# Matmuls over the unnormalised x ahead of four normalised stages of a two-block transformer forward pass

## The reference

```python
def rms(x, g):
    x32 = x.astype(jnp.float32)
    y = x32 * lax.rsqrt(jnp.mean(x32 * x32, axis=-1, keepdims=True) + EPS)
    return (y * g.astype(jnp.float32)).astype(x.dtype)
...
        merged = (gates[:, :, 0] * (y_fox @ w_proj_fox[l])
                  + gates[:, :, 1] * (y_s5 @ w_proj_s5[l])
                  + gates[:, :, 2] * (y_mem @ w_proj_mem[l]))
        x = x + merged @ w_out[l]
    return rms_norm(x, g_final)
...
    for l in range(DEPTH_2):
        ada = c_act @ w_ada[l] + b_ada[l]
        sh1, sc1, gt1, sh2, sc2, gt2 = [a[:, None, :] for a in jnp.split(ada, 6, axis=-1)]

        h = rms(x, g_mix[l]) * (1.0 + sc1) + sh1
        parts = jnp.split(h @ w_in[l], IN_SPLITS, axis=-1)
        ...
        y_a = gqa_attention(qa, ka, va) @ w_branch_a[l]
        ...
        y_b = dilated_attention(qs, kss, vs) @ w_branch_b[l]

        gate_a = jax.nn.sigmoid(parts[3 + 3 * N_B])
        gate_b = jax.nn.sigmoid(parts[4 + 3 * N_B])
        mixed = gate_a * y_a + gate_b * y_b
        x = x + gt1 * (mixed @ w_out[l])

        h2 = rms(x, g_mlp[l]) * (1.0 + sc2) + sh2
        x = x + gt2 * (jnp.square(jax.nn.relu(h2 @ w_ff1[l])) @ w_ff2[l])
```

## Time and profile before

| what | value |
|---|---|
| median of 3 timed executions | 2289.02 us (2288.14 to 2290.26) |
| the profiled execution, its own time | 2291.23 us |
| span of the profiled execution | 2289.4 us |
| mean granted clock of TensorE in it | 0.992 |
| TensorE busy, matmuls | 2249.8 us, 98% |
| GpSimd busy | 1691.9 us, 74% |
| VectorE busy | 1259.3 us, 55% |
| ScalarE busy | 632.8 us, 28% |
| chain of work that ended last | TensorE 85%, GpSimd 6%, VectorE 4%, issue 2%, ScalarE 2%, DMA 1% |
| moved by the DMA queues | 280.87 MB |

### The profile page before, as it was taken

How to read it: one execution, slowest core, us unless ns; L and a number is a source line. 1 busy time by engine, 2 the same in 40 slices (tenths; PEclk the granted TensorE clock), 3 DMA queues, 4 the chain that set the end, 5 groups by cost and what they waited for, 6 DMA issues and landing times.

```text
span 2289.4 us, 31094 instructions
## 1 busy us (share of the span) xinstructions
PE 2249.8 (98%) x11693; PEld 1828.1 (80%) x11693; DVE 1259.3 (55%) x1798; ACT 632.8 (28%) x1286; POOL 1691.9 (74%) x2678
## 2 busy tenths in 40 slices
PE   8999999999999999999999999999999999999999
PEld 6888677788887888777778888878877777888887
DVE  7986345554446665544867576457554456723221
ACT  3233344332224111543223233111144421300000
POOL 7998170867888798344889887889853387899884
PEclk9999999999999899999999999999999999999999
DMA  7456741334455332111545555533321132433221
GB/s 204 129 137 153 268 151 35 116 101 159 159 186 186 111 111 94 50 36 39 164 131 189 174 191 177 184 107 97 100 79 33 29 124 92 154 107 107 92 92 56
DMA packets 268656, 280.87 MB, mean 123 GB/s; under 512 B 29964, under 2 KB 240592, under 8 KB 268508
## 3 DMA queue, kind: packets, MB, share of 16 engines
q1 hardware_dynamic: 249756, 245.86, 34.8%
q10 hardware_dynamic: 18752, 33.03, 4.3%
HBM read 257.87 MB, written 17.85 MB: 120 GB/s over the span
## 4 chain that ended last, share of the span: by engine, by line
PE 85%; POOL 6%; DVE 4%; issue 2%; ACT 2%; DMA 1%; SPq 0%; ACTq 0%; DVEq 0%; POOLq 0%
PE ps L496 46%; PE ps L674 14%; PE ps L2527 4%; PE ps L2528 4%; PE ps L2529 4%; POOL ring_low L272 4%; POOL ring_high L268 3%; PE ps L982 2%; PE ps L1025 2%; PE ps L1001 2%; PE ps L1175 1%; PE ps L1182 1%; PE ps L1158 1%; PE ps L2637 1%; DVE ada_acc L408 1%
## 5 line engine op out<-in xcount | busy, mean ns | idle before, releaser
L272 POOL TENSOR_TENSOR ring_low<-ring,ring_high 128x256 fp32r<-128x256 f32 x1309 | 1039.0, 824 | 28.4
L268 POOL TENSOR_SCALAR ring_high<-ring 128x256 fp32r<-128x256 f32 x1309 | 609.1, 491 | 478.3 <-PE ps L674 170.8
L496 PE MATMUL ps<-hT_high,ring_high 128*128 128x512 f32 x704 | 278.0, 395 | 1.4 <-DVE hT_low L860 1.4
L496 PE MATMUL ps<-hT_low,ring_high 128*128 128x512 f32 x704 | 274.9, 390 | 0.0
L496 PE MATMUL ps<-hT_high,ring_low 128*128 128x512 f32 x704 | 274.0, 389 | 0.0
L674 PE MATMUL ps<-hT_high,ring_high 128*128 128x512 f32 x568 | 234.5, 413 | 3.2 <-POOL ring_low L272 1.4
L674 PE MATMUL ps<-hT_high,ring_low 128*128 128x512 f32 x568 | 225.3, 397 | 0.0
L674 PE MATMUL ps<-hT_low,ring_high 128*128 128x512 f32 x568 | 225.1, 396 | 0.0
L408 DVE TENSOR_REDUCE ada_acc<-ring 128x256 f32<-128x2048 f32 x48 | 188.8, 3933 | 54.8 <-ACT ring L395 54.7
L496 PE MATMUL ps<-hidden_high,ring_high 128*128 128x512 f32 x512 | 201.0, 393 | 0.0
L496 PE MATMUL ps<-hidden_low,ring_high 128*128 128x512 f32 x512 | 199.6, 390 | 0.0
(11 more groups left out here) (401 smaller groups left out, 4030.5 us busy)
## 6 DMA issues: line engine op xcount, KB each, us to landing
ring<-in_w_in_dram SPq DMA_DIRECT2D x75, 1024.0 KB, 5.3
ring<-in_w_ff_dram SPq DMA_DIRECT2D x64, 1024.0 KB, 5.4
ring<-in_w_ada_dram SPq DMA_DIRECT2D x48, 1024.0 KB, 5.4
ring<-in_w_out_dram SPq DMA_DIRECT2D x12, 1024.0 KB, 5.8
scratch_x<-xT ACTq DMA_DIRECT2D x3, 2048.0 KB, 8.2
ring<-in_w_mem_kv_dram SPq DMA_DIRECT2D x4, 1024.0 KB, 5.4
ring<-in_w_branch_a_dram SPq DMA_DIRECT2D x16, 256.0 KB, 4.0
xT<-scratch_x ACTq DMA_DIRECT2D x2, 2048.0 KB, 9.7
```

The source lines that it names most:

```text
L268: ins = nc.gpsimd.tensor_scalar(x(hi), x(raw), 1.0, 1.0, ALU.mult, ALU.mult)
L272: ins = nc.gpsimd.tensor_tensor(x(lo), x(raw), x(hi).bitcast(F32), ALU.subtract)
L496: return nc.tensor.matmul(out[0:rows, bank, cols[0]:cols[1]], lhsT, rhs, start=start, stop=stop)
```

## The change

A normalised and modulated x is `h = x * rstd * gain + shift`, with `rstd` a number per position and `gain` and `shift` numbers per feature. So `h @ W` is `rstd * ((x * gain) @ W) + shift @ W`. The change uses this for a few tiles of each normalised stage:

- During the output tiles in front of a norm, ScalarE rounds up `x * gain` (`Unnormed.round_up`) and VectorE makes its low part (`Unnormed.low_part`), slice by slice as x is updated, and both go into `hT`. One slice behind the last tile is done in the norm stage.
- In the norm stage TensorE works on tiles over this `hT`, 24 products each, and mixes in the products with the shift, 16 matmuls with two columns per tile (`shift_of`; `factors_ahead` makes the high and low part of the shift), the sums (now eight one-column matmuls over `sums` and `last`) and the transposes of the root. The `warm` matmuls are gone. The slices of `hT` are overwritten by the normalised ones when TensorE has used them (`used`). VectorE then multiplies the tiles by `rstd` (`take`).
- In front of layer 0's projections two tiles run ahead: both tiles of the first gate slab `m00ga`. In front of layer 1's, one tile of `m10ga`; the other one runs beside the first four slices of the first projection group, over the normalised x (`beside`). In both layers the gate slab moves ahead of the projections' slabs in the ring, and the stream has 14 gate tiles (336 products) instead of 16, with new paces. `turn_gates` does the tanh of the two at the start of the turn stage.
- In front of both feed-forwards tiles 0 and 1 of `w_ff1` run ahead; tiles 2 and 3 then go slice by slice (`done=2`). The temporary of the norm is in PSUM banks 4 and 6 there.
- The mixing stage waits for the last of the stream at its tile 3 instead of at its entry.
- Five modulation slabs of layer 0 come in the merge, behind the gate slabs with odd numbers 3 to 11, tied to half 0 of that slab; the first block's output stage has two instead of four, and layer 0's output stage none instead of three. The merge has `ada_lag=2` instead of 3.

```diff
@@ plan_slabs
-    def ada(l):
+    def ada(l, half=1):
...
-        key = (last, 1) if K.slabs[last][3] else (last, None)
+        key = (last, half) if K.slabs[last][3] else (last, None)
...
             add(f"merge{mp}{b}g", w, dm, O_GL + D * b, D, part=mp)
+            one = (len(K.slabs) - 1, 1)
+            if 3 * mp + b in (3, 5, 7, 9, 11):
+                ada(0, 0)
             add(f"merge{mp}{b}p", T[pw][0], (0, rows), 0, D, part=mp)
...
         add("out", T["w_out"][0], dm, 0, D, part=i)
-        ada(0)
+        if i < 2:
+            ada(0)
     for l in range(LAYERS):
         w2 = T["w_in_2"][l]
+        add(f"m{l}0ga", w2, dm, 3072, D, part=0)
...
             add(f"out{l}", T["w_out_2"][l], dm, 0, D, part=i)
-            if l == 0 and i < 3:
-                ada(0)
@@ tiles_stage
-                first = 2
+                first = 2 + done
...
-                    for n in range(2):
+                    for n in range(done, done + 2):
@@ new
+def factors_ahead(K, e, shift):
+    v, hi = K.nc.vector, K.shift_two[:, :, 0]
+    K.link(e, "dve_step", v.tensor_copy(hi, shift))
+    K.link(e, "dve_step", v.tensor_tensor(K.shift_two[:, :, 1], shift, hi.bitcast(F32), ALU.subtract))
+class Unnormed:
...
+    def round_up(self, e, k):
+
+        K = self.K
+        K.nc.scalar.activation(K.hT[0][:, k, :], self.src[:, k, :], ACT.Copy, scale=self.gain[:, k:k + 1]
+                               ).then_inc(self.high.sem, 1)
+
+    def low_part(self, e, k):
+
+        K = self.K
+        e.wait_ge(self.high.sem, self.base + k + 1)
+        K.nc.vector.scalar_tensor_tensor(K.hT[1][:, k, :], self.src[:, k, :], self.gain[:, k:k + 1],
+                                         K.hT[0][:, k, :].bitcast(F32), ALU.mult, ALU.subtract).then_inc(self.low.sem, 1)
@@ norm_stage
+            def products_of(k):
+                pe.wait_ge(unnormed.low.sem, unnormed.base + k + 1)
+                for n, t in enumerate(tiles):
+                    if k == 0:
+                        K.weight_here(pe, t[0][5])
+                    for x in range(3 * k, 3 * k + 3):
...
+            def shift_of(n, k):
+
+                for x in (3 * k, 3 * k + 2):
+                    ins = nc.tensor.matmul(ps[:, shift_bank, 2 * n:2 * n + 2], tiles[n][x][3], K.shift_two[:, k, :],
+                                           start=x == 0, stop=x == 3 * KD - 1)
...
+            pe.wait_ge(taken.sem, taken.total - 2)
+            for k in range(KD):
+                products_of(k)
+                if twice is not None:
+                    squared, summed = twice[0]
+                    for h in (2 * k, 2 * k + 1):
+                        shift_of(h // KD, h % KD)
+                    if k == 1:
+                        pe.wait_ge(taken.sem, taken.total)
+                        pe.wait_ge(summed.sem, summed.total)
+                        pe.wait_ge(squared.sem, squared.total - 1)
+                        turn(turn_bank, (sums, last))
+                    if k == 3:
+                        pe.wait_ge(inverted.sem, i0 + 1)
+                        spread_root(root_bank, 4)
+                    if k == 4:
+                        pe.wait_ge(squared.sem, squared.total)
+                        turn(other_bank, (twice[3], twice[4]))
+                    if k == 6:
+                        pe.wait_ge(inverted.sem, i0 + 2)
+                        spread_root(other_bank, 1)
+                else:
+                    for h in range(len(tiles) * k, len(tiles) * (k + 1)):
+                        shift_of(h // KD, h % KD)
+                    if k == (2 if len(tiles) == 1 else 1):
+                        pe.wait_ge(taken.sem, taken.total)
+                        turn(turn_bank, (sums, last))
+                    if k == (4 if len(tiles) == 1 else 2):
+                        pe.wait_ge(inverted.sem, i0 + 1)
+                        spread_root(root_bank, 4)
...
             def round_up(k):
                 e.wait_ge(scaled.sem, s0 + k + 1)
+                e.wait_ge(used.sem, u0 + k + 1)
...
+            K.link(e, "dve_step", v.tensor_copy(rstd[:, :], ps[:, root_bank, :]))
+            e.wait_ge(made.sem, made0 + len(tiles))
+            for n in range(len(tiles)):
+                K.link(e, "dve_step", v.tensor_reduce(K.shift_of[:, n:n + 1], ps[:, shift_bank, 2 * n:2 * n + 2], AX_X, ALU.add))
+                take(e, n, ps[:, tile_banks[n], :], rstd[:, :])
@@ qkv_stage
+                        if g == 0 and beside is not None and k < KD // 2:
+                            if k == 0:
+                                K.weight_here(pe, beside[0][0][5])
+                            for j in (2 * k, 2 * k + 1):
+                                pe.wait_ge(arriving[0].sem, arriving[1] + j + 1)
+                                for _, _, _, lhsT, rhs, _, start, stop in beside[0][3 * j:3 * j + 3]:
+                                    ins = nc.tensor.matmul(K.ps[:, beside[1], :], lhsT, rhs, start=start, stop=stop)
@@ layer
+    def turn_gates(e):
+        e.wait_ge(gates_scaled.sem, gates_scaled.total)
+        for n in range(2):
+            shift = {"bias": K.half_shift[:, n:n + 1]} if n < ahead else {}
+            nc.scalar.activation(gates[n], scaled_gates[n][:, :], ACT.Tanh, scale=0.5, **shift).then_inc(gates_turned.sem, 1)
...
-                    [72 + 9 * i for i in range(18)] + [240, 252])
+                    [72] + [85 + 8 * i for i in range(17)] + [220, 226])
...
-                         [(252, 252, 274)] + [(278 + 14 * i, 284 + 14 * i, 288 + 14 * i) for i in range(7)] + [(376, 382, 384)])
+                         [(226, 226, 246)] + [(249 + 10 * i, 254 + 10 * i, 256 + 10 * i + 8 * (i == 6)) for i in range(7)] + [(328, 334, 336)])
...
-    tiles_stage(K, tiles, 2, dve=mix_dve, also=mix_high, waits={(0, 0): (al.sem, al0 + 4), (0, 12): (yl.sem, yl0 + 2)})
+    tiles_stage(K, tiles, 2, dve=mix_dve, also=mix_high, tensor_entry={x: y for x, y in before.items() if x != "stream"},
+                entry_at=(3, {"stream": before["stream"]}), waits={(0, 0): (al.sem, al0 + 4), (0, 12): (yl.sem, yl0 + 2)})
...
-    tiles_stage(K, column_tiles(K, K.first[f"out{l}"], KD, KD, split), 1, dve=out_dve, ahead=mlp_gain,
+    tiles_stage(K, column_tiles(K, K.first[f"out{l}"], KD, KD, split), 1, dve=out_dve, also=out_high, ahead=mlp_gain,
                 arriving=(xl, xl0, before, 5))
...
+    after[5] = 1
...
     def ff_act(e, n, ps):
+        if n < 2:
+            e.wait_ge(first_scaled.sem, scaled0 + n + 1)
+            return nc.scalar.activation(rel[:, n, :], rel[:, n, :], ACT.Relu, bias=K.shift_of[:, n:n + 1])
```

## The result

The changed kernel takes 2303.84 us (2302.14 to 2306.41), against 2288.86 us before on the same chips: a ratio of 1.0063, 95% interval 1.0051 to 1.0075. It is 15 us slower where 7 us faster was forecast. Its profiled execution took 2306.41 us, with a span of 2304.6.

The account below looks back on a forecast made before the run. TensorE bounds (busy 2249.8 of 2289.4 us), GpSimd second. Terms 20.4 + 1.4 + 1.5 + 1.6 + 2.9 - 10.9 - 9.7 = 7.2 us faster, so 2281.8 us; 8 in 10 range 2270 to 2292.

Parts of the forecast that it names:

- part 6: Merge and first projections: five moved modulation slabs land second, 5 us from the merge; a loss of 9.7 us in all.
- Rival (b): Merge: the ring of three slabs starves if the second slab lands 5.4 us late; 12 us slower, 2294; chance 0.18.
- its sign of being right: Merge: TensorE's stops there would sum to over 12 us.
- Part 1: Attention stages: two gate tiles per layer leave the streams, 21.8 us less 1.4 for disturbed steps; gain 20.4 us.
- rival (c): Attention stages: exponentials and VectorE's pass set the wide step, its 10 us over both layers are lost; 2291; chance 0.12.
- part 2: Entry of the mixing stage: TensorE no longer waits for the last gate before its first tile; gain 1.4 us.
- Part 3: Both feed-forward gates, last product before to tile 4: 27.1 us plus 1.75 wait; gains 1.5 (layer 0) and 1.6 (layer 1).
- price of a two-column matmul: Stages with tiles ahead: each such matmul for the shift takes 0.12 us, bounds half and twice.
- Part 5: Layer 1's projections: second group 39.4 us after the last product before, instead of 28.5; a loss of 10.9 us.
- The first projections: Layer 0's projections: the second column group starts at 791.0 against 781.29; a loss of 9.7 us.
- The half clock is gone, since TensorE has work there: First projections: the half clock of 745 to 762 would vanish, as TensorE has tiles to work on.
- Part 4: Layer 0's output stage: without three modulation slabs a 2.16 us stop and three pairs of transposes go; gain 2.9 us.

Follow-up runs that it names:

- run 4: The changed kernel with the transfers of the five moved modulation slabs cut to one eighth: 2306.01 us (one execution).
- run 12: The changed kernel with the transfer cut to one eighth in the ordinary modulation slab of the same five pairs, not the moved one: 2289.29 us (one execution).
- run 11: The changed kernel with each of the five moved modulation slabs in front of its gate slab, not behind it: 2292.65 us, ratio 1.0011.
- run 7: The kernel of run 6 with all two-column matmuls for the shift in one block behind the products ahead: 2309.43 us.
- run 15: The kernel of run 10 with layer 1's projections and gate stream as before the change: 2288.16 us, ratio 0.9991.
- Run 2: The kernel before with only the five modulation slabs moved into the merge, with its earlier turn: 2304.62 us, ratio 1.0064.
- run 10: The changed kernel with all modulation slabs where they were before and the old norm stage for layer 0's feed-forward: 2288.38 us, ratio 0.9989.
- run 1: The changed kernel with the merge's turn of a modulation slab put back to three tiles after its scaling, not two: 2306.00 us, ratio 1.007.
- run 5: The changed kernel with each modulation slab in the merge scaled, summed and turned one tile later: 2314.82 us, ratio 1.0107.
- run 6: The changed kernel without slabs moved into the merge: one more in the stage before it, three beside layer 0's mixing stage: 2306.21 us, ratio 1.007.
- run 3: The changed kernel without slabs moved into the merge: three in the first output stage, four beside layer 0's mixing stage: 2300.71 us, ratio 1.0049.
- run 8: The kernel of run 6 with three quarters of the two-column matmuls for the shift left out: 2298.60 us.

## Why the prediction was wrong

**The step that failed is part 6,** the price of the five modulation slabs moved into the merge. It put the second of two transfers 2 us later, let the merge absorb half, and came to 5 us; the merge took 24.7. Two things were wrong. It asked only when the wanted *weights* land, and looked at each of the five places by itself; it never wrote down which slot each slab falls into. With four slabs on three slots the ordinary modulation slab, which it did not look at, was the late one (runs 4 and 12). Exchanging two places gave 12.1 us of the 24.7 back (run 11); the other half is tied to the number of slabs, and how it divides between slots, landings and low parts stays open. And it named TensorE's slack of about 1 us for a pair, but not ScalarE's place in the order: behind a late slab stand the tanh of the next tile, VectorE's product of that tile, and the sum that TensorE must turn.

**Rival (b)** had the right place and sign, and its sign of being right came true: the stops of the merge sum to more than 12 us. But its price was 12 us more than the 5, less than the 24.7, so that the measured 2303.84 lies beyond its 2294 too. Its mechanism was wrong: it expected weights to starve, with the point of decision at a landing 3.5 us later. In the change TensorE's stops of the merge stand in front of the turns of sums. It had a chance of 0.18. The argument against it, that slabs issued together have landed in time so far, was about the landing and not about the slot.

**Part 1** was right in kind: the steps are 5.0 and 7.0 us as forecast, so rival (c) is out. With part 2 it was too small by 3.3 and 3.5 us a layer, since the stops at the end of the wide attention (1.5 us) and at the entry of mixing (1.0 and 1.1, part 2) went as well; of 3.2 and 3.4 us of stops in that stretch 0.3 are left. The mixing stages took 0.5 each back.

**Part 3** held in layer 0, 28.97 us against 28.85 forecast, but by two misses that cancel. The second half was split 1.7 us after T0, just as forecast (1.75), so the 2.7 us for six low parts beside GpSimd came true; but three products over the first half go ahead of it, 0.68 us that the forecast left out, and the wait was 1.05. In its place the sums took 1.8 us, not 0.95: the row of eight in the earlier trace rows is four matmuls, two records each, and the change has eight matmuls, 16 records. The rule of the Trainium skill (SBUF — State Buffer, "Who interferes with whom"), a full exclusion, would by the prediction's working have split that half 3.5 us after T0; the traces show 1.7 and do not agree with it. In layer 1 the gain was lost to 3.4 us at half clock, which the forecast, with TensorE at work all the time, had ruled out. The price of a two-column matmul was right: four of them and the delay of the product behind take 0.46 us, 0.115 each.

**Part 5**: 41.16 us against 39.4; the stop for the third pair of halves is 2.05 us, forecast 2.1. The 1.8 us missing are mostly the half clock again: run 7, without it there, took 39.2. The sums, 0.8 us longer than forecast, are in it too. That this part takes back what its stream gained was right, and run 15 confirms it.

**The first projections** came out at 50.0 us from T0. The forecast's 791.0 is 49.2 behind the old T0, but 5 of that are the merge's; from its own T0 it is 44.1, so they are 5.8 us too long. The wait for the second half was not what was missing: 2.5 us, not the 4.7 of the forecast (the low parts cost GpSimd 1.4 us there: the half ends 3.3 us after T0, before 1.9). But TensorE ran 13.6 us at half clock behind it, which loses 6.8, and the two blocks of sums need 1.8 us each at full clock, not 0.95. "The half clock is gone, since TensorE has work there" is refuted. Run 2 shows a second miss: 6.3 us of the 15.2 before were the wait for the last sums of slabs, which moving two slabs away from the output stage frees without any tile ahead.

**Part 4** held, 3.3 us against 2.9; part 2 can't be told apart from what the attentions gave.

## What to carry to other kernels

Where slabs pass through a ring in order, write out for every edit of the list which slab takes over which slot, and when that slot is released; one slab more in a period equal to the number of slots ties slabs together that had nothing to do with each other. A side job that stands in three engines' program orders costs by its latest arrival, not by its busy time. And of a gain that depends on TensorE's clock, measure several executions: the profiled one of run 10 promised 6 us, the median kept 2. A total of waits, like ScalarE's 81.2 and 80.2 us in runs 4 and 12, does not price a change; the chain through each stop of the bounding engine does.

## What the runs showed of the hardware

TensorE's granted clock fell while it was not idle. Windows of the changed kernel (window, sum, busy of PE, PEld, DVE, ACT, POOL, then the granted clock):

```profile
771.00:781.00 10.00, 10.00 (x37) 8.90 (x37) 1.40 (x3) 2.12 (x4) 8.01 (x14) 0.51 0.36 108
...
1542.00:1546.00 4.00, 4.00 (x17) 3.48 (x18) 0.18 (x1) 0.26 (x1) 3.92 (x9) 0.57 0.01 4
1945.00:1949.00 4.00, 4.00 (x16) 3.44 (x17) 0.23 (x2) 0.26 (x1) 3.92 (x9) 0.57 0.00 0
1175.50:1192.00 16.50, 15.61 (x93) 13.34 (x93) 10.32 (x15) 4.40 (x7) 11.02 (x19) 1.00 0.40 128
```

In the first three PE is busy for the whole window and the clock is near 0.5, the 1.2 GHz level; in all three the matmuls before were products mixed with two-column and one-column ones. In front of the first window TensorE had also stood still for 2.5 us, in front of the third for 0.9. The fourth is the same mixture, and the clock stayed at 1.00: in layer 0's feed-forward it fell in runs 1, 5 and 6 and not in the change and in runs 3 and 11. In layer 1's it fell in every execution with all the short matmuls but that of run 10. With three quarters of them gone it fell in neither feed-forward (run 8). But the kernel before, which has none of two columns, shows 0.50 with PE busy for the whole of 1926.0 to 1929.4, at the same place in layer 1. So the short matmuls cannot be the only cause, and what decides it when the instructions are the same stays open.
